# Layer normalisation on one core: the root computed on 128 tokens by 4 and spread by products with scaled identities

## The chip, the core and the metric

The kernel runs on one NeuronCore of a Trainium2 chip. The core has TensorE (PE, matrix products into PSUM; PEld is its weight load), VectorE (DVE), ScalarE (ACT), GpSimd (POOL) and the queue engine SyncE (SP), all working on a shared on-chip memory, SBUF. Time is the device time of one execution in microseconds (us), and the figure compared is the median of several runs.

## The reference

Two transformer blocks are computed for one sequence of 512 tokens with 1024 features. The first block has two layers, and each layer normalises twice, so there are four layer normalisations:

```python
def _layer_norm(x, g, b):
    xf = x.astype(jnp.float32)
    mu = jnp.mean(xf, -1, keepdims=True)
    var = jnp.mean(jnp.square(xf - mu), -1, keepdims=True)
    y = (xf - mu) * lax.rsqrt(var + NORM_EPS)
    return (y * g.astype(jnp.float32) + b.astype(jnp.float32)).astype(x.dtype)
...
    for i in range(DEPTH):
        ...
        x = _layer_norm(DN_ALPHA * x + m, ln1_g[i], ln1_b[i])
        x = _layer_norm(DN_ALPHA * x + _sq_relu_mlp(x, w_up[i], w_down[i]), ln2_g[i], ln2_b[i])
        gate = jax.nn.sigmoid(x @ ple_w_gate[i] + ple_b_gate[i])
        x = x + gate * (p[i] @ ple_w_proj[i])
```

The second block (attention variants, gates, a gated feed-forward part, root-mean-square norms) is not touched.

## The kernel before

Activations are held feature-major: the 128 partitions are features, a row holds the 512 tokens, and 8 such tiles (j = 0 to 7) make the 1024 features. Every large product is split in three: the weight tile and the activation are each written as a rounded high part (WH, XH) and a low part (WL, XL), and high by high, low by high and high by low are summed in a PSUM bank. ACT rounds the weights (L375), DVE subtracts to get the low part (L381, L391), each engine in its own written-out order with semaphores between them.

The four normalisations are called ln1_0, ln2_0, ln1_1 and ln2_1. Their helpers are `ln_pe`, `ln_act`, `ln_pool` and `ln_dve`, one for each engine. Since features lie on partitions, the sums over features come from TensorE: a product with a 128x128 block of ones (ONES) gives the sum for each of the 512 tokens, repeated on all 128 partitions.

- While the residual tiles ACC[:, j] arrive, ACT squares each into X[:, j] (L733) and POOL sums tiles 0 to 6 of both (L787 the values, into SUM1, which the trace calls SM; L791 the squares, into SUM2, which is PT for ln1 and SCR for ln2).
- `ln_pe` makes four f32 products of 512 columns: SUM1 and the last ACC tile into PSUM bank 7 (L697, L699), SUM2 and the last squared tile into bank 6 (L702, L704).
- ACT turns bank 7 into the negative mean (L759, signals `mn`) and squares it (L761). From `mn` on POOL subtracts the mean from tiles 1 to 7, seven operations in a row (L794), and DVE from tile 0 (L798).
- DVE forms the variance for 128x512 elements (L801, L803), ACT takes logarithm and exponential (L763, L765) and a square (L767), DVE makes one Newton step (L806, L808) and leaves the root in bank 6. Then DVE scales the tiles (L814), ACT writes the high part XH with the bias (L775) and DVE the low part XL (L818).
- Meanwhile TensorE runs `proj`, 24 products of 512 columns (four banks, 6 products each, L1231 to L1233) that don't need the normalised tiles. Then comes `lin_pair`: two weight tiles at a time, 48 products (L1294, L1295, L1298), each group as soon as its XH and XL tile are there.

## Time and profile before

| what | value |
|---|---|
| median of 3 runs | 2225.22 us (2224.31 to 2225.51) |
| profiled execution, whole time | 2223.27 us |
| its span from first to last instruction | 2221.4 us |
| TensorE busy | 2173.6 us, 98% of the span |
| VectorE busy | 1237.8 us, 56% |
| ScalarE busy | 896.4 us, 40% |
| GpSimd busy | 220.8 us, 10% |
| mean granted TensorE clock | 1.000 |

Some 1.9 us lie around the span. The shares are averages over a long program; in a normalisation, which takes some ten microseconds, the engines wait for each other in another way than the averages tell.

### The profile page before, as it was taken

Reading aid. Unit: us, or ns where it says so; the run is one execution under the profiler, and the core shown is the slowest. Engines: PE = TensorE matmul, PEld = TensorE weight load, DVE = VectorE, ACT = ScalarE, POOL = GpSimd, SP = SyncE. Lnnn points to the kernel's source line nnn. Section 1 sums busy time; section 2 is a strip of 40 time slices with the busy share of each in tenths; the row PEclk is TensorE's granted clock in tenths of the full one; section 3 lists DMA queues with packets and bytes.
Section 4 is the critical chain, followed back from the end, with each engine's and each line's share of the span. In section 5 each row is a group of like instructions: output and inputs, shape, how many; then the busy total and the mean of one; then the engine's idle time right before and its main releaser. Section 6 shows DMA issues by size and latency. Waiting matters only on the chain.

```text
span 2221.4 us, 27724 instructions
## 1 busy us (share of the span) xinstructions
PE 2173.6 (98%) x10141; PEld 1718.9 (77%) x10141; DVE 1237.8 (56%) x1991; ACT 896.4 (40%) x1498; POOL 220.8 (10%) x145
## 2 busy tenths in 40 slices
PE   8999999999999999999999999999999999999998
PEld 6777788888777777788888777678778787888887
DVE  5676643343474554643344377388489678542554
ACT  4565443233254544433243264432543443321332
POOL 0000400001400001400001320133000231000000
PEclk9999999999999999999999999999999999999999
DMA  6113233333223331333333244123222142333231
GB/s 175 27 46 105 76 94 104 91 98 104 76 77 102 98 96 48 94 95 104 86 98 104 62 135 109 45 86 105 78 61 78 50 121 67 104 104 95 86 104 67
DMA packets 351395, 197.45 MB, mean 89 GB/s; under 512 B 20896, under 2 KB 340141, under 8 KB 351294
## 3 DMA queue, kind: packets, MB, share of 16 engines
q1 hardware_dynamic: 350882, 196.03, 30.9%
q8 instruction: 64, 1.05, 0.2%
q14 instruction: 37, 0.30, 0.0%
q10 hardware_dynamic: 412, 0.07, 0.0%
HBM read 193.93 MB, written 2.14 MB: 88 GB/s over the span
## 4 chain that ended last, share of the span: by engine, by line
PE 85%; DVE 8%; issue 3%; ACT 3%; DMA 0%; POOL 0%; DVEq 0%; SPq 0%; ACTq 0%; POOLq 0%
PE PB L411 20%; PE PB L413 20%; PE PB L412 20%; PE PB L494 3%; PE PB L1407 2%; PE PB L1408 2%; PE PB L1409 2%; PE PB L540 2%; PE PB L513 2%; PE PB L1622 2%; PE PB L1623 2%; PE PB L1624 2%; DVE ATT L2996 1%; DVE WL L381 1%; PE PB L1294 1%
## 5 line engine op out<-in xcount | busy, mean ns | idle before, releaser
L375 ACT ACTIVATE WH<-RAW 128x1024 fp32r<-128x1024 f32 (+3 forms) x355 | 358.3, 1013 | 367.7 <-PE PB L413 273.4
L411 PE MATMUL PB<-XH,WH 128*128 128x512 f32 x1232 | 487.4, 396 | 5.3 <-DVE X L2431 1.3
L413 PE MATMUL PB<-XH,WL 128*128 128x512 f32 x1232 | 480.4, 390 | 0.0
L412 PE MATMUL PB<-XL,WH 128*128 128x512 f32 x1232 | 479.7, 389 | 0.0
L391 DVE TENSOR_TENSOR WL<-RAW,WH 128x1024 fp32r<-128x1024 f32 x172 | 220.7, 1284 | 148.5 <-ACT WH L375 146.6
L411 PEld LDWEIGHTS PB<-XH,WH 128*128 128x128 f32 x1232 | 231.0, 187 | 59.6 <-issue 3.3
L413 PEld LDWEIGHTS PB<-XH,WL 128*128 128x128 f32 x1232 | 230.8, 187 | 49.5
L412 PEld LDWEIGHTS PB<-XL,WH 128*128 128x128 f32 x1232 | 231.1, 188 | 47.1 <-issue 0.7
L381 DVE TENSOR_TENSOR WL<-RAW,WH 128x1024 fp32r<-128x1024 f32 (+2 forms) x163 | 195.6, 1209 | 104.7 <-ACT WH L375 104.0
L413 PE MATMUL PB<-HH,WL 128*128 128x512 f32 x512 | 199.3, 389 | 0.0
L411 PE MATMUL PB<-HH,WH 128*128 128x512 f32 x512 | 199.2, 389 | 0.0
L412 PE MATMUL PB<-HL,WH 128*128 128x512 f32 x512 | 199.2, 389 | 0.0
L2614 DVE TENSOR_SCALAR HR<-PB 128x512 f32<-128x512 f32 x64 | 44.2, 691 | 143.7 <-PE PB L413 143.7
L2038 ACT ACTIVATE HS<-HR 128x512 f32<-128x512 f32 x64 | 40.5, 633 | 190.7 <-DVE HR L2614 190.7
L627 ACT ACTIVATE PT<-PB 128x256 f32<-128x256 f32 (+3 forms) x160 | 65.4, 411 | 120.4 <-PE PB L513 120.4
L411 PEld LDWEIGHTS PB<-HH,WH 128*128 128x128 f32 x512 | 96.1, 188 | 20.0
L413 PEld LDWEIGHTS PB<-HH,WL 128*128 128x128 f32 x512 | 96.1, 188 | 20.0
L412 PEld LDWEIGHTS PB<-HL,WH 128*128 128x128 f32 x512 | 96.1, 188 | 19.9
L787 POOL TENSOR_TENSOR SM<-ACC 128x512 f32<-128x512 f32 x4 | 5.2, 1296 | 1056.6 <-DVE ACC L2600 569.1
L1407 PE MATMUL PB<-XH,WH 128*128 128x512 f32 x256 | 102.9, 402 | 0.4 <-ACT RS L2152 0.4
L1409 PE MATMUL PB<-XH,WL 128*128 128x512 f32 x256 | 99.9, 390 | 0.0
L1408 PE MATMUL PB<-XL,WH 128*128 128x512 f32 x256 | 99.8, 390 | 0.0
(514 smaller groups left out, 3530.2 us busy)
## 6 DMA issues: line engine op xcount, KB each, us to landing
RAW<-in_w_up SPq DMA_DIRECT2D x64, 512.0 KB, 4.0
RAW<-in_w_down SPq DMA_DIRECT2D x64, 512.0 KB, 3.9
RAW<-in_w_ffn_gate_up SPq DMA_DIRECT2D x44, 512.0 KB, 3.8
RAW<-in_w_gate SPq DMA_DIRECT2D x32, 512.0 KB, 4.0
RAW<-in_od_w_in SPq DMA_DIRECT2D x24, 512.0 KB, 6.3
RAW<-in_w_in SPq DMA_DIRECT2D x24, 512.0 KB, 4.1
RAW<-in_w_ffn_down SPq DMA_DIRECT2D x22, 512.0 KB, 3.3
RAW<-in_ple_w_gate SPq DMA_DIRECT2D x16, 512.0 KB, 4.0
```

The costliest lines, as they stand in the source:

```text
L375: act.activation(WH[:, s, 0:nb], RAW[:, s, 0:nb], ACT.Copy).then_inc(hi_done[s], 1)
L381: eng.tensor_tensor(WL[:, s, 0:nb], RAW[:, s, 0:nb], WH[:, s, 0:nb].bitcast(F32), ALU.subtract).then_inc(lo_done[s], 1)
L391: dve.tensor_tensor(WL[:, s], RAW[:, s], WH[:, s].bitcast(F32), ALU.subtract).then_inc(lo_done[s], 1)
L411: pe.matmul(PB[b][0:m, 0:n], WH[:, s, k, 0:m], rh[:, kk, :], start=kk == 0, stop=False)
L412: pe.matmul(PB[b][0:m, 0:n], WH[:, s, k, 0:m], rl[:, kk, :], start=False, stop=False)
L413: x = pe.matmul(PB[b][0:m, 0:n], WL[:, s, k, 0:m], rh[:, kk, :], start=False, stop=kk == last)
L494: xs[e] = pe.matmul(PB[2 + e][:, lo:lo + w], q[:, qb * P:qb * P + P], k[:, ks[0] * P:ks[0] * P + w], start=True, stop=plain)
L513: x = pe.transpose(PB[4 + e][:, c * P:c * P + P], PR[:, e, c * P:c * P + P], ID[:])
L627: done(act.activation(PT[:, e, ks[0]:ks[0] + len(ks), qb * P:qb * P + P], PB[4 + e][:, 0:len(ks) * P].rearrange("p (j q) -> p j q", q=P), ...
L1407: pe.matmul(PB[m % 2][:], WH[:, n % 4, k], XH[:, k], start=k == 0, stop=False)
L1408: pe.matmul(PB[m % 2][:], WH[:, n % 4, k], XL[:, k], start=False, stop=False)
L1409: x = pe.matmul(PB[m % 2][:], WL[:, n % 4, k], XH[:, k], start=False, stop=k == DT - 1)
```

## The change

The variance and the root are computed in another layout: tokens on the 128 partitions, 4 columns (one for each group of 128 tokens). A product whose stationary operand is a 128x128 block of the data and whose moving operand is one column of ones gives the sums for 128 tokens in one PSUM column. Sixteen such products are made for each normalisation (SUM1, SUM2, the last ACC tile, the last squared tile, four blocks each); the two 512-column products of the squares are gone, the two of the mean stay. The chain from variance to root is done on 128x4 elements in STAT. The root then goes back over the features: each of its four columns scales the identity matrix (ID) into a 128x128 block of TMP, two on DVE and two on ACT, and a product of ONES with that block repeats the 128 roots on all partitions. These four products (`ln_spread`) stand in the middle of `proj`, after its first 12 products.

```diff
         def ln_pe(pe, key):
+            sum2, last = SUM2[key[:3]], ACC[:, DT - 1]
+            pe.wait_ge(sem["sum7"], cnt.value("sum7", (key, DT - 2)))
+            for k in range(TT):
+                pe.matmul(PB[6][:, TT + k:TT + k + 1], SUM1[:, k * P:k * P + P], ONES[:, 0:1], start=k == 0, stop=False, skip_group_check=True)
+            pe.wait_ge(sem["sum7q"], cnt.value("sum7q", (key, DT - 2)))
+            for k in range(TT):
+                pe.matmul(PB[6][:, k:k + 1], sum2[:, k * P:k * P + P], ONES[:, 0:1], start=False, stop=False, skip_group_check=True)
             def mean():
-                pe.wait_ge(sem["sum7"], cnt.value("sum7", (key, DT - 2)))
                 pe.matmul(PB[7][:], ONES[:], SUM1, start=True, stop=False)
                 evac_of(pe, M_LN[key] + DT - 1)
-                return pe.matmul(PB[7][:], ONES[:], ACC[:, DT - 1], start=False, stop=True)
+                for k in range(TT):
+                    pe.matmul(PB[6][:, TT + k:TT + k + 1], last[:, k * P:k * P + P], ONES[:, 0:1], start=False, stop=False, skip_group_check=True)
+                return pe.matmul(PB[7][:], ONES[:], last, start=False, stop=True)
             pe_misc(pe, ("mean", key), mean)
-            pe.wait_ge(sem["sum7q"], cnt.value("sum7q", (key, DT - 2)))
-            pe.matmul(PB[6][:], ONES[:], SUM2[key[:3]], start=True, stop=False)
             pe.wait_ge(sem["sqr"], cnt.value("sqr", (key, DT - 1)))
-            done(pe.matmul(PB[6][:], ONES[:], X[:, DT - 1], start=False, stop=True), "varb", key)
+            for k in range(TT):
+                x = pe.matmul(PB[6][:, k:k + 1], X[:, DT - 1, k * P:k * P + P], ONES[:, 0:1], start=False, stop=True, skip_group_check=True)
+            done(x, "varb", key)
+
+        def ln_spread(pe, key):
+            for c, k in enumerate(DIAG_ORDER):
+                wait(pe, "diag_a" if c % 2 else "diag_d", (key, k))
+                x = pe.matmul(PB[6][:, k * P:k * P + P], ONES[:], TMP[:, k * P:k * P + P], start=True, stop=True)
+            done(x, "rootb", key)
...
+        DIAG_ORDER = (0, 2, 1, 3)
+        R0, ROOT = STAT[:, 12:16], STAT[:, 20:24]
         def ln_act(act, key, b, st=None):
...
-            done(act.activation(MEANSQ[key[:3]], MEAN, ACT.Square), "m2", key)
             act.wait_ge(sem["ln_v"], cnt.value("ln_v", key))
-            done(act.activation(RS[:], TMP[:], ACT.Ln), "rs_ln", key)
+            done(act.activation(R0, STAT[:, 8:12], ACT.Ln, bias=EPS5[:]), "rs_ln", key)
...
-            done(act.activation(RS[:], RS[:], ACT.Exp, scale=-0.5), "chain_a", ("rs", key))
-            act.wait_ge(sem["chain_a"], cnt.value("chain_a", ("rs", key)))
-            done(act.activation(PB[7][:], RS[:], ACT.Square), "rs_exp", key)
+            done(act.activation(R0, R0, ACT.Exp, scale=-0.5), "rs_exp", key)
+            act.wait_ge(sem["root"], cnt.value("root", key))
+            for k in DIAG_ORDER[1::2]:
+                done(act.activation(TMP[:, k * P:k * P + P], ID[:], ACT.Copy, scale=ROOT[:, k:k + 1]), "diag_a", (key, k))
...
         def ln_dve(dve, key, g, b):
...
-            done(dve.scalar_tensor_tensor(TMP[:], PB[6][:], 1.0 / D, MEANSQ[key[:3]], ALU.mult, ALU.subtract), "chain_d", ("v", key))
-            done(dve.tensor_scalar(TMP[:], TMP[:], 0.0, 1e-5, ALU.max, ALU.add), "ln_v", key)
+            link(dve.tensor_scalar(q, PB[6][:, TT:2 * TT], -1.0 / D, None, ALU.mult), "m")
+            link(dve.tensor_tensor(q, q, PB[6][:, TT:2 * TT], ALU.mult), "mm")
+            link(dve.tensor_tensor(q, q, PB[6][:, 0:TT], ALU.add), "dv")
+            done(dve.tensor_scalar(v, q, 1.0 / D, 0.0, ALU.mult, ALU.max), "ln_v", key)
             dve.wait_ge(sem["ln_v"], cnt.value("ln_v", key))
+            link(dve.tensor_scalar(v_eps, v, 1e-5, None, ALU.add), "ve")
             dve.wait_ge(sem["rs_exp"], cnt.value("rs_exp", key))
-            done(dve.scalar_tensor_tensor(PB[7][:], PB[7][:], -0.5, TMP[:], ALU.mult, ALU.mult), "chain_d", ("n2", key))
-            done(dve.scalar_tensor_tensor(PB[6][:], PB[7][:], 1.5, RS[:], ALU.add, ALU.mult), "misc_free", ("mean", key))
+            link(dve.tensor_tensor(q, R0, R0, ALU.mult), "n1")
+            link(dve.scalar_tensor_tensor(q, q, -0.5, v_eps, ALU.mult, ALU.mult), "n2")
+            done(dve.scalar_tensor_tensor(ROOT, q, 1.5, R0, ALU.add, ALU.mult), "root", key)
+            dve.wait_ge(sem["root"], cnt.value("root", key))
+            for k in DIAG_ORDER[0::2]:
+                done(dve.tensor_scalar(TMP[:, k * P:k * P + P], ID[:], ROOT[:, k:k + 1], None, ALU.mult), "diag_d", (key, k))
             dve.wait_ge(sem["misc_free"], cnt.value("misc_free", ("mean", key)))
+            dve.wait_ge(sem["rootb"], cnt.value("rootb", key))
...
                 for i in range(4):
+                    if i == 2:
+                        ln_spread(pe, key)
                     for k in range(2):
```

This is what TensorE issues for ln1_0 before, from the end of the layer's output product on; the last row is the first product of `proj`.

```order
L697 MATMUL PB<-SM,ONES 128x512 [waits sum7,misc_free]
L699 MATMUL PB<-ACC,ONES 128x512 [waits evac1]
L702 MATMUL PB<-PT,ONES 128x512 [waits sum7q]
L704 MATMUL PB<-X,ONES 128x512 [waits sqr]
L1231 MATMUL PB<-PTH,WH 128x512 [waits ptev,pt_lo,lo_done0]
```

And this is what it issues in the changed kernel at the same place, and then in the middle of `proj`.

```order
L697 MATMUL PB<-ONES,SM 128x1 [waits sum7]
L700 MATMUL PB<-ONES,PT 128x1 [waits sum7q]
L703 MATMUL PB<-SM,ONES 128x512 [waits misc_free]
L706 MATMUL PB<-ONES,ACC 128x1 [waits evac1]
L707 MATMUL PB<-ACC,ONES 128x512
L711 MATMUL PB<-ONES,X 128x1 [waits sqr]
L1261 MATMUL PB<-PTH,WH 128x512 [waits ptev,pt_lo,lo_done0]
...
L718 MATMUL PB<-TMP,ONES 128x128 [waits diag_d]
L718 MATMUL PB<-TMP,ONES 128x128 [waits diag_a]
```

Each 128x1 row stands for the first of four products. Eight of them, and the wait for the summed squares (`sum7q`), now come ahead of the mean's products, four more between those two. The four spreading products wait for the scaled identities with the second half of `proj` queued behind them.

This is what DVE issues for ln1_0 before, from the mean to the first scaled tiles.

```order
L798 SCALAR_TENSOR_TENSOR ACC<-PB,ACC 128x512 [waits mn]
L801 SCALAR_TENSOR_TENSOR TMP<-PB,PT 128x512 [waits m2,varb]
L803 TENSOR_SCALAR TMP<-TMP 128x512 [waits chain_d]
L806 SCALAR_TENSOR_TENSOR PB<-PB,TMP 128x512 [waits rs_exp,ln_v]
L808 SCALAR_TENSOR_TENSOR PB<-PB,RS 128x512 [waits chain_d]
L814 SCALAR_TENSOR_TENSOR ACC<-ACC,VEC,PB 128x512 [waits misc_free]
```

And this is DVE in the changed kernel.

```order
L815 SCALAR_TENSOR_TENSOR ACC<-PB,ACC 128x512 [waits mn]
L822 TENSOR_SCALAR STAT<-PB 128x4 [waits varb]
L823 TENSOR_TENSOR STAT<-STAT,PB 128x4 [waits chain_d]
L824 TENSOR_TENSOR STAT<-STAT,PB 128x4 [waits chain_d]
L825 TENSOR_SCALAR STAT<-STAT 128x4 [waits chain_d]
L827 TENSOR_SCALAR STAT<-STAT 128x4 [waits ln_v]
L829 TENSOR_TENSOR STAT<-STAT 128x4 [waits rs_exp,chain_d]
L830 SCALAR_TENSOR_TENSOR STAT<-STAT 128x4 [waits chain_d]
L831 SCALAR_TENSOR_TENSOR STAT<-STAT 128x4 [waits chain_d]
L834 TENSOR_SCALAR TMP<-ID,STAT 128x128 [waits root]
L834 TENSOR_SCALAR TMP<-ID,STAT 128x128
L841 SCALAR_TENSOR_TENSOR ACC<-ACC,VEC,PB 128x512 [waits rootb,misc_free]
```

Four wide operations became ten narrow ones. Before, one of the four (L803) has all its operands in SBUF; of the ten, the last seven (L825 to L834) have.

## Rows read from the trace of the kernel before

**Rows 1.** The page: engines' busy time, and the chain that ended last.
```profile
PE 2173.6 (98%) x10141; PEld 1718.9 (77%) x10141; DVE 1237.8 (56%) x1991; ACT 896.4 (40%) x1498; POOL 220.8 (10%) x145
PE 85%; DVE 8%; issue 3%; ACT 3%; DMA 0%; POOL 0%; DVEq 0%; SPq 0%; ACTq 0%; POOLq 0%
```

**Rows 2.** Waits of PE: total us, times, longest.
```profile
PE PB L1294 <- ACT XH L775: 8.0, 7, 1.9
```

**Rows 3.** Timeline of ln2_0: start, length (us), engine, line, tiles, [idle before].
```profile
597.19 1.02 PE L697 MATMUL PB<-SM,ONES 128*128 128x512 f32 x2
...
598.25 1.13 PE L699 MATMUL PB<-ACC,ONES 128*128 128x512 f32 x2
...
599.21 1.02 PE L702 MATMUL PB<-SCR,ONES 128*128 128x512 f32 x2
...
599.41 0.60 ACT L759 ACTIVATE SM<-PB 128x512 f32<-128x512 f32 x1 [0.56 <-PE PB L699]
...
600.04 0.69 DVE L798 SCALAR_TENSOR_TENSOR ACC<-PB,ACC 128x512 f32<-128x512 f32 x1 [1.85 <-ACT SM L759]
600.07 1.02 PE L704 MATMUL PB<-X,ONES 128*128 128x512 f32 x2
...
600.08 8.96 POOL L794 TENSOR_TENSOR ACC<-ACC,SM 128x512 f32<-128x512 f32 x7 [9.17 <-ACT SM L759]
...
606.44 1.41 DVE L814 SCALAR_TENSOR_TENSOR ACC<-ACC,VEC,PB 128x512 f32<-128x512 f32 x2
...
608.05 1.54 DVE L818 SCALAR_TENSOR_TENSOR XL<-ACC,VEC,XH 128x512 fp32r<-128x512 f32 x1 [0.20 <-ACT XH L775]
608.09 0.47 PE L1294 MATMUL PB<-XH,WH 128*128 128x512 f32 x1 [1.51 <-ACT XH L775]
...
619.19 0.84 PE L1298 MATMUL PB<-XL,WH 128*128 128x512 f32 x3
```

**Rows 4.** Timeline of ln1_0, the same columns.
```profile
236.70 1.27 POOL L791 TENSOR_TENSOR PT<-PT,X 128x512 f32<-128x512 f32 x1
...
239.56 8.93 POOL L794 TENSOR_TENSOR ACC<-ACC,SM 128x512 f32<-128x512 f32 x7 [1.59 <-ACT SM L759]
...
247.91 0.47 PE L1294 MATMUL PB<-XH,WH 128*128 128x512 f32 x1 [1.88 <-ACT XH L775]
...
258.60 0.84 PE L1298 MATMUL PB<-XL,WH 128*128 128x512 f32 x3
```

**Rows 5.** Single lines: length min/median/max in ns, first and last start; then POOL's timeline.
```profile
L803 DVE TENSOR_SCALAR TMP<-TMP x4: 1043/1049/1294, 241.3 to 1275.3; 128x512 f32<-128x512 f32 x4
L2845 DVE TENSOR_TENSOR SC<-SC,CHK x3: 294/1264/2385, 1464.2 to 1467.9; 128x128 f32<-128x128 f32 x3
1464.02 3.69 POOL L381 TENSOR_TENSOR WL<-RAW,WH 128x1024 fp32r<-128x1024 f32 x2 [6.35 <-ACT WH L375]
```

**Rows 6.** Timeline of PE where small f32 products follow 512-column ones.
```profile
1716.40 0.39 PE L1408 MATMUL PB<-XL,WH 128*128 128x512 f32 x1
1716.62 0.39 PE L1409 MATMUL PB<-XH,WL 128*128 128x512 f32 x1
1716.85 3.73 PE L1492 MATMUL PB<-XX 128*128 128x128 f32 x32
1720.34 0.48 PE L1407 MATMUL PB<-XH,WH 128*128 128x512 f32 x1
```

**Rows 7.** Timeline of a 128x1 root chain at the program's end.
```profile
2208.05 0.29 ACT L2367 ACTIVATE STAT<-STAT 128x1 f32<-128x1 f32 x1
...
2208.60 0.15 DVE L3182 SCALAR_TENSOR_TENSOR STAT<-STAT 128x1 f32<-128x1 f32 x1
2208.79 0.16 DVE L3184 TENSOR_TENSOR STAT<-STAT 128x1 f32<-128x1 f32 x1
```

**Rows 8.** Clock: last product; window (length, busy, clock, DMA, GB/s); one line's lengths.
```profile
2215.01 0.39 PE L1624 MATMUL PB<-WL,H 128*128 128x512 f32 x1
2220.00:2220.50 0.50, 0.00 (x0) 0.97 0.99 377
L1244 PE MATMUL PB<-ID,XIN x32: 272/421/448, 6.9 to 12.8; 128*128 128x128 f32 x32
```

More of the change, by code:

```diff
@@ L92 @@
  topk hsp hg_x hg_prod hg_read hg_e hg_d hg_o hg_small hx mn m2 varb ln_v x_full sum7q pj pj_free memsum cross xsum
- asum ysum h_up quad mvt yt yo ot_in xt_in z r_tok merge os brf var_out var_in dn dn_free gain_in tok_ss tok_y tok_rt""".split()
+ asum ysum h_up quad mvt yt yo ot_in xt_in z r_tok merge os brf root diag_a diag_d rootb var_out var_in dn dn_free gain_in tok_ss tok_y tok_rt""".split()
 def program(nc, known, t):
@@ L215, in program @@
         SUM2 = {"ln1": PT[:, 0, 0], "ln2": SCR[:, 1]}
-        MEANSQ = {"ln1": PT[:, 0, 1], "ln2": SCR[:, 0]}
         assert max(end_a, end_b, end_c + 4096) <= nc.sbuf_usable_end, (end_a, end_b, end_c, nc.sbuf_usable_end)
@@ L759, in ln_act @@
             done(act.activation(MEAN, PB[7][:], ACT.Copy, scale=-1.0 / D), "mn", key)
-            act.wait_ge(sem["mn"], cnt.value("mn", key))
-            done(act.activation(MEANSQ[key[:3]], MEAN, ACT.Square), "m2", key)
             act.wait_ge(sem["ln_v"], cnt.value("ln_v", key))
-            done(act.activation(RS[:], TMP[:], ACT.Ln), "rs_ln", key)
+            done(act.activation(R0, STAT[:, 8:12], ACT.Ln, bias=EPS5[:]), "rs_ln", key)
             act.wait_ge(sem["rs_ln"], cnt.value("rs_ln", key))
-            done(act.activation(RS[:], RS[:], ACT.Exp, scale=-0.5), "chain_a", ("rs", key))
-            act.wait_ge(sem["chain_a"], cnt.value("chain_a", ("rs", key)))
-            done(act.activation(PB[7][:], RS[:], ACT.Square), "rs_exp", key)
+            done(act.activation(R0, R0, ACT.Exp, scale=-0.5), "rs_exp", key)
+            act.wait_ge(sem["root"], cnt.value("root", key))
+            for k in DIAG_ORDER[1::2]:
+                done(act.activation(TMP[:, k * P:k * P + P], ID[:], ACT.Copy, scale=ROOT[:, k:k + 1]), "diag_a", (key, k))
             if key[:3] == "ln2":
@@ L797, in ln_dve, with link @@
             dve.wait_ge(sem["mn"], cnt.value("mn", key))
-            dve.scalar_tensor_tensor(ACC[:, 0], PB[7][:], -1.0 / D, ACC[:, 0], ALU.mult, ALU.add)
+            done(dve.scalar_tensor_tensor(ACC[:, 0], PB[7][:], -1.0 / D, ACC[:, 0], ALU.mult, ALU.add), "misc_free", ("mean", key))
+            v, q, v_eps = STAT[:, 8:12], STAT[:, 16:20], STAT[:, 24:28]
+            def link(ins, step):
+                done(ins, "chain_d", (step, key))
+                dve.wait_ge(sem["chain_d"], cnt.value("chain_d", (step, key)))
@@ L799, in ln_dve @@
             dve.wait_ge(sem["varb"], cnt.value("varb", key))
-            dve.wait_ge(sem["m2"], cnt.value("m2", key))
-            done(dve.scalar_tensor_tensor(TMP[:], PB[6][:], 1.0 / D, MEANSQ[key[:3]], ALU.mult, ALU.subtract), "chain_d", ("v", key))
-            dve.wait_ge(sem["chain_d"], cnt.value("chain_d", ("v", key)))
-            done(dve.tensor_scalar(TMP[:], TMP[:], 0.0, 1e-5, ALU.max, ALU.add), "ln_v", key)
+            link(dve.tensor_scalar(q, PB[6][:, TT:2 * TT], -1.0 / D, None, ALU.mult), "m")
@@ L807, in ln_dve @@
-            dve.wait_ge(sem["chain_d"], cnt.value("chain_d", ("n2", key)))
-            done(dve.scalar_tensor_tensor(PB[6][:], PB[7][:], 1.5, RS[:], ALU.add, ALU.mult), "misc_free", ("mean", key))
+            link(dve.tensor_tensor(q, R0, R0, ALU.mult), "n1")
+            link(dve.scalar_tensor_tensor(q, q, -0.5, v_eps, ALU.mult, ALU.mult), "n2")
+            done(dve.scalar_tensor_tensor(ROOT, q, 1.5, R0, ALU.add, ALU.mult), "root", key)
+            dve.wait_ge(sem["root"], cnt.value("root", key))
@@ L1218, in proj @@
             def proj(l, o0):
+                key = f"ln{1 if o0 == 0 else 2}_{l}"
                 s, u = st.slot(0)
```

## The prediction

> **What bounds the kernel now.** I read the page first: TensorE is busy for 98% of the span and carries 85% of the last chain [rows 1], so time is won only where TensorE stops, or where it has less to do. Then I read its waits: the largest is that of `lin_pair` for the first normalised tile, 8.0 us in 7 places [rows 2]. So a shorter way from the last residual tile to the first XH tile could win some 1.5 to 1.9 us in each of four normalisations, no more [rows 3, 4]. Then I read the timeline of a normalisation, ln2_0 in full and ln1_0 for what differs. The reader is to see three things there. The four products of the sums take 0.86 us each (L702 to L704). The mean's signal starts POOL on seven subtractions, 8.96 us without a pause, or 1.28 us each; call the start of these P, 600.08 for ln2_0. And `lin_pair` starts at 608.09, P + 8.0 (P + 8.35 in ln1_0). All the root work of DVE lies within POOL's seven operations.
>
> The view that matters most for this change is that of single DVE lines beside POOL [rows 5]. L803 takes 1.05 us, where L798, as wide, takes 0.69. Its start at 241.3 plus 1.05 is 242.35; POOL's second operation ends at 239.56 + 2 x 1.28 = 242.1, and L803 ends 0.25 after it. It has waited for POOL. L818 shows the same: it takes 1.54 us from 608.05, POOL ends at 609.04, and it ends 0.55 later [rows 3]. L2845 shows what happens to several such operations in a row: three of one size (128x128) take 2.385, 1.264 and 0.294 us, beside two POOL operations, the second of which ends at 1467.7. The first of them ends at 1466.6, and so has waited for POOL's first operation. The second ends some 0.15 after 1467.7: POOL's second operation got in between them. Only the third, started at 1467.9 with POOL idle, shows its own length. So two DVE operations that both read SBUF twice don't pass one POOL operation together: the two engines take turns.
>
> The Trainium skill has this as a rule (SBUF — State Buffer, Who interferes with whom): a DVE instruction with two SBUF inputs, or one in a 2-port mode, and a GpSimd instruction lock a shared port pair for their whole length, and the later one blocks fully. The trace agrees, with the 1.264 us of the second L2845 beside 0.294. The Trainium skill (VectorE: DVE Perf Modes, Mode 2×_2P) puts single-source operations in SBUF with an even length among those that lock; no row here shows that for a 4-column one.
>
> **The change, step by step.** The new chain on DVE has seven operations that read and write SBUF only: the variance, its eps, n1, n2, the root, and the two scaled identities. By themselves they are short: links of a chain of one column stand 0.19 us apart [rows 7].
>
> Sums on TensorE: eight loads of f32 weights make a group of four one-column products (two passes each). Thirty-two such passes of 128 columns take 3.49 us, 0.109 each [rows 6], and a pass needs a load of its own whether one column or 128 follow. I take 0.109, so a group costs 0.87 us. Two groups and the products SUM1, then a third group, then the last ACC tile: the mean is later by three groups, 2.6 us. In ln2_0, 0.2 of that is slack, since L699 waited until 598.25 for the last tile where L697 was done at 598.05: 2.4. In ln1_0 the squares' sum, which stood behind the mean, now stands ahead of it, and POOL ends it at 237.97 [rows 4], some 0.3 after the first group: 2.9. So P moves by 2.4 and 2.9.
>
> From P on: DVE takes tile 0 (0.69), then three short operations that read PSUM, so the variance is asked for at P + 1.26, just at POOL's first boundary. Whether it gets in there or at the next, the seven operations meet seven POOL operations: if the first is early, the last goes at the seventh boundary; if not, the last finds POOL done. Seven boundaries of 1.28 are 8.96; with what DVE itself takes in between, the last scaled identity is ready at P + 9.3. ACT's logarithm, exponential and its two identities (0.55 us from L2367 to L3182 [rows 7]) are hidden by these waits. TensorE then makes the last two of the four spreading products: four passes of 0.109, with the signal 0.5, P + 9.8. Then come the 12 products of `proj` that are queued behind them, at 0.227 each [rows 6], 2.7 us: `lin_pair` starts at P + 12.5. The first XH tile is no longer what it waits for: that is 1.65 us after the first L814 [rows 3], and so 1 us before TensorE is through with `proj`.
>
> Sum for ln1_0: 12.5 - 8.35 + 2.9 = 7.05 us later. For ln2_0: 12.5 - 8.0 + 2.4 = 6.9. The third resembles the first without its POOL wait and the fourth the second; I take 6.9 for each. Together 27.8 us. Against it stands the start of `lin_pair`: its 48 products are worth 10.9 us, and they took 11.4 in ln1_0 (247.91 to 258.60 and three products) and 11.8 in ln2_0 (608.09 to 619.19 and three), the stalls behind a late L818. With POOL done and two tiles ahead these go: 2 x (0.45 + 0.85) = 2.6 saved. This leaves 25 us.
>
> The clock: TensorE has nothing from the end of the first half of `proj`, about P + 2.7, until the first scaled identity, at the sixth or seventh boundary, P + 8.0 or P + 9.3. That is 5.3 to 6.6 us. At the program's end the granted clock falls within the window 2220.0 to 2220.5, 5.1 us after the last product [rows 8], from 2.4 to 1.2 GHz. So in some or all of the four the rest of `proj` runs at the lower clock. How slow it is shows at the start, where transposes take 421 ns in the median and 272 at best, until about 12 us, 5 us after the first. Bounds: nothing, or 5 us at half speed, 2.5 us. I take 1.5 for each, 6 together, since the gap is only a little longer than what the end shows. Total 31 us: 2223.27 + 31 = 2254 for the profiled execution, and 2256 for the median, which lies 2 us above it.
>
> **Rivals.**
> *Only two-input operations take turns.* The 4-column variance and eps pass beside POOL; for it speaks that no row shows a narrow single-source operation held. Then five operations wait, the chain ends one boundary earlier, P + 8.0, and the gap on TensorE is 3.9 us, too short for the clock by the row of the end [rows 8]: 25 - 4 x 1.3 = 20, 2245.
>
> *Short operations are not held at all.* For it: L2845 is 128 columns wide, these 4. Against it: its wait is the whole POOL operation, whatever its own length. Then the root is ready by P + 2.6, the identities by P + 3.3, the spreading ends near P + 3.7, and `lin_pair` starts at P + 6.4, 0.8 later than now for ln2_0 with P moved by 2.4. POOL now ends 2.4 us later as well, so one or two more L818 wait for it. About 1 us each: 2229.
>
> *Faster.* If nothing is held, TensorE's work alone decides: 32 loads of a pass x and 0.87 for the spreading come, two products (1.72) and the stall of 1.5 to 1.9 go. The two are even at x = 0.08 us. If a one-column pass costs less than that, the kernel gains; at 0.05 it is 1 us each, 2221. Against it: no f32 load in the trace is so quick behind another, and it needs the rival before it.
>
> *The clock stays low for longer*, into `lin_pair`, or a stall of the same sort comes up elsewhere: above 2266.
>
> **How the numbers follow.** Turns with POOL as forecast 0.66, of which with a clock that never falls (2250) about a third; two-input operations only 0.13; nothing held 0.11; faster 0.04; over 2266 0.06. The forecast's own range is 2248 to 2266. The range reaches down into the second case, 2240, and up to the clock's upper bound, four times 2.5 (2260) with a few us for the mis-sized groups: 2240 to 2265, about 0.8. A measurement of this kernel tells 0.2%, 4.5 us, from no change. The case "nothing held" lies at that border, half in, half out: faster 0.04, same 0.07, slower 0.89.
>
> **What would show it.** In the profile after, POOL's seven subtractions start 2.4 to 2.9 us later in their normalisation than before; beside them the 4-column DVE lines have medians near 1.2 us where their own length is 0.15; the last identity ends 9.3 us after POOL's start; TensorE has a gap of 5 to 7 us in the middle of `proj`, ended by an identity on DVE; `lin_pair` no longer waits for XH; the clock is below 1.0 in windows behind some gaps. The prediction is wrong if the 4-column lines take 0.15 us beside POOL, or if POOL doesn't get in between them.

## The result, and the profile after

The changed kernel takes 2256.35 us (median of 4 executions, 2255.99 to 2257.37) against 2224.89 before (2224.31 to 2225.51), measured side by side: 1.0144 of the time before, with a 95% interval of 1.013 to 1.0159. It is 31.5 us slower. The profiled execution has a span of 2254.6 us, where it was 2221.4.

The page after: busy times, and the clock in 40 slices.

```profile
PE 2197.3 (97%) x10283; PEld 1744.9 (77%) x10285; DVE 1253.1 (56%) x2015; ACT 891.4 (40%) x1498; POOL 219.4 (10%) x145
PEclk9999899999999999999999999999999999999999
```

Its waits of PE. The row of [rows 2] is gone from the list, and this one heads it:

```profile
PE PB L718 <- DVE TMP L834: 16.6, 4, 4.6
```

`lin_pair` no longer waits for its first XH tile; the spreading products wait for the identities that DVE scales, four times, at most 4.6 us. What holds DVE is seen in its single lines (ns, min/median/max; first and last start), in the order of the chain:

```profile
L822 DVE TENSOR_SCALAR STAT<-PB x4: 151/151/163, 244.7 to 1301.6; 128x4 f32<-128x4 f32 x4
L825 DVE TENSOR_SCALAR STAT<-STAT x4: 190/190/1123, 245.2 to 1302.2; 128x4 f32<-128x4 f32 x4
L827 DVE TENSOR_SCALAR STAT<-STAT x4: 1199/1217/1217, 246.4 to 1302.4; 128x4 f32<-128x4 f32 x4
L829 DVE TENSOR_TENSOR STAT<-STAT x4: 1182/1182/1200, 247.6 to 1303.7; 128x4 f32<-128x4 f32 x4
L831 DVE SCALAR_TENSOR_TENSOR STAT<-STAT x4: 1183/1186/1186, 250.1 to 1306.1; 128x4 f32<-128x4 f32 x4
L834 DVE TENSOR_SCALAR TMP<-ID,STAT x8: 273/1250/1308, 251.3 to 1308.5; 128x128 f32<-128x128 f32 x8
```

L822 and L827 do the same kind of work on the same 128x4 elements. The one reads PSUM and takes 0.15 us; the other reads and writes SBUF and takes 1.22. The timeline of ln2_0 after, to be laid beside [rows 3], shows why:

```profile
606.80 0.95 PE L697 MATMUL PB<-ONES,SM 128*128 128x1 f32 x8
607.61 1.03 PE L700 MATMUL PB<-ONES,SCR 128*128 128x1 f32 x8
...
612.07 8.65 POOL L811 TENSOR_TENSOR ACC<-ACC,SM 128x512 f32<-128x512 f32 x7 [11.54 <-ACT SM L777]
...
613.20 0.19 DVE L825 TENSOR_SCALAR STAT<-STAT 128x4 f32<-128x4 f32 x1
613.43 1.22 DVE L827 TENSOR_SCALAR STAT<-STAT 128x4 f32<-128x4 f32 x1
...
614.61 0.39 PE L1263 MATMUL PB<-PTH,WL 128*128 128x512 f32 x1
614.68 1.18 DVE L829 TENSOR_TENSOR STAT<-STAT 128x4 f32<-128x4 f32 x1
...
617.11 1.19 DVE L831 SCALAR_TENSOR_TENSOR STAT<-STAT 128x4 f32<-128x4 f32 x1
618.33 2.47 DVE L834 TENSOR_SCALAR TMP<-ID,STAT 128x128 f32<-128x128 f32 x2
...
619.63 2.44 PE L718 MATMUL PB<-TMP,ONES 128*128 128x128 f32 x8 [4.64 <-DVE TMP L834]
...
621.73 0.77 PE L1261 MATMUL PB<-PTH,WH 128*128 128x512 f32 x1
```

POOL's seven operations take 8.65 us, 1.236 each, so its second ends at 614.54 and its third at 615.78. L827 ends at 614.65 and L829 at 615.86: each narrow operation ends 0.1 us behind one of POOL's. The second identity ends at 620.80, behind the seventh (620.72). TensorE ran out of products at 615.00 and waits until 619.63.

The clock in that stage, and in ln1_0 (windows: length, then busy time of PE, PEld, DVE, ACT, POOL, then granted clock, DMA share and GB/s):

```profile
616.00:618.00 2.00, 0.00 (x0) 0.00 (x0) 1.97 (x2) 0.00 (x0) 2.00 (x2) 1.00 0.00 0
618.00:619.00 1.00, 0.00 (x0) 0.00 (x0) 0.96 (x2) 0.67 (x2) 1.00 (x2) 0.84 0.00 0
622.00:624.00 2.00, 2.00 (x6) 1.53 (x5) 1.60 (x3) 1.02 (x2) 0.00 (x0) 0.50 0.00 0
626.00:628.00 2.00, 2.00 (x11) 1.61 (x10) 2.00 (x4) 0.84 (x2) 0.00 (x0) 1.00 0.00 0
...
238.00:240.00 2.00, 2.00 (x13) 1.52 (x13) 0.00 (x0) 0.00 (x0) 0.00 (x0) 0.95 0.00 0
240.00:242.00 2.00, 2.00 (x7) 1.55 (x8) 0.00 (x0) 0.00 (x0) 0.00 (x0) 0.50 0.00 0
```

In ln2_0 the clock falls to half (1.2 GHz) inside the gap, after 618, and `proj` runs at it until 625.5, which is almost all of its rest. In ln1_0 it falls at another place as well: at 239.8, while TensorE is shown busy with the one-column products. The prediction has nothing of that.

The four normalisations hold the whole loss. From the first product of the sums to the end of `lin_pair` (its last product counted with the 0.227 us at which products follow each other) they took 22.4, 22.7, 22.75 and 22.65 us (90.5 together) and now take 32.3, 30.4, 30.6 and 30.6 (123.9): 33.5 us more by the unrounded times, where the span grew by 33.2. These sums of four stages are used below for each kernel.

### The profile page after: what moved, and what is told of

The parts are those of the page before. It is cut to its first block, busy times and chain, and to the rows that moved or that the text cites. A ratio compares the mean times of both kernels' runs of the same rounds, so it can differ in the third digit from the quotient of the medians.

```text
span 2254.6 us, 28030 instructions
## 1 busy us (share of the span) xinstructions
PE 2197.3 (97%) x10283; PEld 1744.9 (77%) x10285; DVE 1253.1 (56%) x2015; ACT 891.4 (40%) x1498; POOL 219.4 (10%) x145
## 4 chain that ended last, share of the span: by engine, by line
PE 86%; DVE 8%; issue 3%; ACT 2%; DMA 0%; POOL 0%; DVEq 0%; SPq 0%; ACTq 0%; POOLq 0%
PE PB L410 20%; PE PB L412 20%; PE PB L411 20%; PE PB L493 2%; PE PB L1437 2%; PE PB L1438 2%; PE PB L1439 2%; PE PB L539 2%; PE PB L512 2%; PE PB L1654 2%; PE PB L1653 2%; PE PB L1652 2%; PE PB L1324 1%; PE PB L1325 1%; PE PB L1328 1%
```

## The experiments

### The turns with POOL

**POOL starts later (e1_pool_waits).** One line of the changed kernel: POOL's subtractions wait for the last identity of DVE instead of the mean.

```diff
         def ln_pool(pool, key, b):
...
-            pool.wait_ge(sem["mn"], cnt.value("mn", key))
+            pool.wait_ge(sem["diag_d"], cnt.value("diag_d", (key, 1)))
```

> The changed kernel with one edit: POOL starts its seven subtractions only when DVE has written both scaled identities. Every DVE operation is the same. Turn-taking theory: the 4-column lines L825 to L831 take 0.15 to 0.19 us each (1.18 to 1.22 before this edit), the identities 0.27, and the gap in the middle of proj shrinks from about 5 us to 1.3 or less, so the clock stays at 1.0 there. POOL and DVE's L845 now take turns later, 1 to 3 us for each normalisation. Time 2226 to 2240, middle 2233. Rival, the narrow chain is slow by itself (ten linked operations and two hops to ACT): the lines keep about 1.2 us or the gap stays over 4 us, and the time stays above 2250.

Measured: 2237.31 us (2234.48 to 2238.55), 1.0059 [1.0043, 1.0074] of the time before; four stages 99.9 us. Two of its lines:

```profile
L829 DVE TENSOR_TENSOR STAT<-STAT x4: 162/164/165, 246.2 to 1287.4; 128x4 f32<-128x4 f32 x4
L845 DVE SCALAR_TENSOR_TENSOR XL<-ACC,VEC,XH x32: 737/1118/1673, 251.9 to 1302.6; 128x512 fp32r<-128x512 f32 x32
```

With POOL idle the same instruction takes 0.164 us, not 1.182. So the length that it had was POOL's. In ln2_0 the pause in the middle of `proj` is gone, and the stage takes 24.3 us instead of 30.4; some 2 of these 6 are the clock, which no longer falls behind a gap there (e3 below). The kernel gets 19 us back. In ln1_0 the clock still falls in the sums, at 241.3. Part of the price is moved: POOL's work now lies beside L845, whose median goes from 0.74 to 1.12.

**Half as wide on POOL (e8_pool_halves).** The same subtractions as 14 operations of 256 columns.

```diff
-                done(pool.tensor_tensor(ACC[:, j], ACC[:, j], MEAN, ALU.add), "cen", (key, j))
+                pool.tensor_tensor(ACC[:, j, 0:256], ACC[:, j, 0:256], MEAN[:, 0:256], ALU.add)
+                done(pool.tensor_tensor(ACC[:, j, 256:512], ACC[:, j, 256:512], MEAN[:, 256:512], ALU.add), "cen", (key, j))
```

> The changed kernel with POOL's seven subtractions cut into fourteen of 256 columns. Nothing on DVE, ACT or TensorE is edited. Turn-taking theory: a turn costs one POOL operation, so the narrow DVE lines fall from 1.18 to about 0.6 us, the chain from POOL's start to the second identity from 8.7 to about 4.7 us, the gap in proj closes but for 1.5 us and the clock stays up behind it. L845 then meets POOL's second half. About 5.5 us less in each normalisation, 2234 (2230 to 2240). Rival, a narrow operation waits for POOL's whole queue or for a fixed time: the lines keep 1.2 us and the time stays at 2255 to 2258.

Measured: 2239.71 us (2239.29 to 2241.15), 1.0072 [1.0055, 1.0088]; four stages 105.0 us. The chain's lines, one number further on, and POOL's:

```profile
L830 DVE TENSOR_TENSOR STAT<-STAT x4: 647/659/659, 247.1 to 1290.1; 128x4 f32<-128x4 f32 x4
L831 DVE SCALAR_TENSOR_TENSOR STAT<-STAT x4: 646/646/656, 247.8 to 1290.8; 128x4 f32<-128x4 f32 x4
L811 POOL TENSOR_TENSOR ACC<-ACC,SM x28: 712/734/1237, 244.3 to 1296.2; 128x256 f32<-128x256 f32 x28
```

The DVE instructions are unchanged, and go from 1.18 to 0.65 us with POOL's. A wait for POOL's whole instruction explains both; a fixed cost of a narrow operation explains neither. The second identity ends 5.6 us after POOL's start in ln2_0, where it was 8.7. The clock still falls in ln1_0's sums and, in ln1_1, at 929.5, behind a gap of 2.1 us.

**The chain through PSUM (e2_psum_chain).** POOL starts as in the change. Each DVE operation has at most one operand in SBUF; the square of R0 and all four identities are ACT's.

```diff
-            link(dve.tensor_tensor(q, q, PB[6][:, 0:TT], ALU.add), "dv")
-            done(dve.tensor_scalar(v, q, 1.0 / D, 0.0, ALU.mult, ALU.max), "ln_v", key)
+            link(dve.tensor_tensor(qp, q, PB[6][:, 0:TT], ALU.add), "dv")
+            done(dve.tensor_scalar(v, qp, 1.0 / D, 0.0, ALU.mult, ALU.max), "ln_v", key)
...
-            link(dve.tensor_scalar(v_eps, v, 1e-5, None, ALU.add), "ve")
+            link(dve.tensor_scalar(v_eps, qp, 1.0 / D, 1e-5, ALU.mult, ALU.add), "ve")
...
-            link(dve.tensor_tensor(q, R0, R0, ALU.mult), "n1")
-            link(dve.scalar_tensor_tensor(q, q, -0.5, v_eps, ALU.mult, ALU.mult), "n2")
-            done(dve.scalar_tensor_tensor(ROOT, q, 1.5, R0, ALU.add, ALU.mult), "root", key)
+            link(dve.scalar_tensor_tensor(qp, PB[6][:, 8:12], -0.5, v_eps, ALU.mult, ALU.mult), "n2")
+            done(dve.scalar_tensor_tensor(ROOT, qp, 1.5, R0, ALU.add, ALU.mult), "root", key)
...
```

> The changed kernel with the chain's operands placed so that no DVE operation between the mean and the root reads SBUF twice or goes from SBUF to SBUF (two of its small arrays lie in PSUM, ACT squares the root's first estimate), and with all four scaled identities on ACT. POOL starts at the mean as in the changed kernel. Turn-taking theory: the narrow lines take about 0.15 to 0.2 us beside POOL, the four identities 0.35 each on ACT, the gap in proj is 1 to 2 us, the clock stays up there; L845 still waits for POOL at first, as in the kernel before. Per normalisation some 2 us more than before the change, 2233 (2229 to 2238). Rival, narrow operations are held by POOL wherever their operands lie: lines near 1.2 us, over 2248.

Measured: 2233.78 us (2232.25 to 2235.44), 1.0042 [1.0026, 1.0057]; four stages 99.6 us, three of them 23.9; in ln1_0 the clock fell in the sums, at 239.8.

```profile
L830 DVE TENSOR_SCALAR STAT<-PB x4: 161/161/161, 245.3 to 1284.7; 128x4 f32<-128x4 f32 x4
L832 DVE SCALAR_TENSOR_TENSOR PB<-PB,STAT x4: 170/170/171, 246.2 to 1285.6; 128x4 f32<-128x4 f32 x4
L814 POOL TENSOR_TENSOR ACC<-ACC,SM x28: 1270/1288/1743, 243.7 to 1290.9; 128x512 f32<-128x512 f32 x28
```

Beside POOL operations of 1.29 us the chain now runs at its own length. The single operands tell the two rules apart: L827 of the changed kernel has one operand, in SBUF, and waits; L830 here has one, in PSUM, and doesn't. The Trainium skill (SBUF — State Buffer, Who interferes with whom) says that a DVE instruction with at most one SBUF input, outside the 2-port modes, doesn't contend with GpSimd. The trace agrees, with 0.16 to 0.17 us.

**Two identities back on DVE (e6_psum_dve_ids).** e2, with the two even blocks scaled by DVE again, from ID in SBUF into TMP in SBUF.

```diff
...
-            for k in DIAG_ORDER:
+            for k in DIAG_ORDER[1::2]:
...
+            for k in DIAG_ORDER[0::2]:
+                done(dve.tensor_scalar(TMP[:, k * P:k * P + P], ID[:], ROOT[:, k:k + 1], None, ALU.mult), "diag_d", (key, k))
```

> As the kernel with the chain's operands in PSUM, but two of the four identities are made by DVE again, from SBUF to SBUF. Turn-taking theory: these two, and only these, take turns with POOL, 1.2 us each where they take 0.28 alone; the spreading ends 1 to 1.5 us later than there, and L845 meets less of POOL afterwards: some 1 us more per normalisation, 2237 (2235 to 2241). Rival, ACT's four identities in a row were the slow part: the same time as there or less, 2231 to 2234.

Measured: 2239.64 us (2237.26 to 2239.94), 1.0066 [1.0049, 1.0083]; four stages 104.8 us.

```profile
L836 DVE TENSOR_SCALAR TMP<-ID,STAT x8: 962/1284/1322, 250.4 to 1292.8; 128x128 f32<-128x128 f32 x8
```

Two turns are back, 1.28 us for work of 0.28, and the stages are 5.2 us longer than in e2. In ln2_0 `lin_pair` starts 8.4 us after POOL instead of 7.0, and is itself 0.6 shorter: 0.85 in all, and as much in ln1_1. That is the price of the two turns. In ln1_0 and ln2_1 the difference is 1.6 and 1.9, and there the clock has a part: it was low in ln1_0 from 239.5 to 253.1, where in e2 it was back at 250.1, and in ln2_1 it fell in the sums, as it didn't in e2.

**The mean's products first (e4_mean_first).** The changed kernel with the groups on SUM1 and SUM2 moved behind the products of the mean. This takes back more than half of the delay of POOL's start and leaves the turns.

```diff
...
             pe_misc(pe, ("mean", key), mean)
+            for k in range(TT):
+                pe.matmul(PB[6][:, TT + k:TT + k + 1], SUM1[:, k * P:k * P + P], ONES[:, 0:1], start=False, stop=False, skip_group_check=True)
+            pe.wait_ge(sem["sum7q"], cnt.value("sum7q", (key, DT - 2)))
+            for k in range(TT):
+                pe.matmul(PB[6][:, k:k + 1], sum2[:, k * P:k * P + P], ONES[:, 0:1], start=False, stop=False, skip_group_check=True)
...
```

> The changed kernel with the one-column groups of SUM1 and SUM2 moved behind the mean's two products (the group of the last tile stays ahead of the second). The products are the same. The mean, and with it POOL's start, comes 1.6 us earlier, the variance at the same time as in the changed kernel. Turn-taking theory: two of POOL's seven operations are over before the first DVE operation that needs SBUF twice, so the last identity escapes a turn, the chain ends about 1.2 us earlier than in the changed kernel: 2251 (2247 to 2253). Rival, the order of the groups is what the path pays for in full, 1.6 us each: 2249.5; if POOL's start sets nothing: 2256.

Measured: 2246.03 us (2243.84 to 2248.7), 1.0102 [1.0085, 1.0119], below the expected range; four stages 111.1 us. POOL starts 3.8 us after the first product in ln2_0 instead of 5.3. The chain starts later against POOL, so five of its operations wait for a turn where six did, and the identities find POOL done:

```profile
L834 DVE TENSOR_SCALAR TMP<-ID,STAT x8: 281/284/288, 249.1 to 1299.0; 128x128 f32<-128x128 f32 x8
```

The last identity ends 13.0 us after the stage's first product, where it was 14.0: an earlier POOL by 1.5 us is worth 1.0. But the stage is 3.0 us shorter (27.45 for 30.4), and `lin_pair` starts 12.8 us after POOL, where it was 14.3. The other 2 us are the clock's. In all four stages it fell in the sums or right behind them, and in ln2_0 it was up again when the rest of `proj` ran, which in the change runs at half clock:

```profile
610.00:614.00 4.00, 4.00 (x11) 3.03 (x11) 3.83 (x6) 0.50 (x2) 4.00 (x4) 0.50 0.00 0
616.00:618.00 2.00, 1.57 (x11) 1.49 (x12) 0.83 (x4) 1.90 (x3) 0.03 (x1) 1.00 0.00 0
```

The slow part then lies in the first half of `proj`, and even so TensorE is through with that half 1.4 us before the first identity comes.

### The clock

**Work in the gap (e3_fill).** The changed kernel with five 512-column products, whose result is not used, ahead of the spreading products.

```diff
                     if i == 2:
+                        wait(pe, "misc_free", ("mean", key))
+                        for c in range(5):
+                            pe.matmul(PB[7][:], ONES[:], X[:, c], start=True, stop=True)
                         ln_spread(pe, key)
```

> The changed kernel with five f32 products of 512 columns put into PSUM bank 7, which nobody reads, ahead of the spreading products, 4.3 us of work in TensorE's gap of 4.6 us. Nothing waits for them. If the low clock after the gap is a part of the loss, the granted clock stays 1.0 behind the gaps of ln2_0, ln1_1 and ln2_1, the second half of proj takes 0.227 us a product and the time falls by 2 to 3 us in each of the three, to 2248 (2246 to 2251); ln1_0, where the clock falls ahead of the gap, may keep its loss. Rival, the clock costs nothing because the next phase waits for XL anyway: 2255 to 2257.

Measured: 2253.23 us (2252.22 to 2254.37), 1.0128 [1.0113, 1.0144]; four stages 119.0 us. The median is above the expected 2246 to 2251, and only one of the three stages did what was expected. In ln2_0 the clock stays up, and the stage takes 28.25 us instead of 30.43: the clock's price behind the gap is 2.2 us. But ln1_1 and ln2_1 gain only 0.5 each, since there the clock now falls ahead of the gap. Windows of ln2_0, ln1_1 and ln2_1:

```profile
612.00:616.00 4.00, 4.00 (x14) 2.30 (x13) 3.87 (x4) 0.50 (x2) 4.00 (x4) 1.00 0.00 0
620.00:624.00 4.00, 4.00 (x20) 3.31 (x19) 3.50 (x6) 2.03 (x3) 0.00 (x0) 1.00 0.01 2
926.00:930.00 4.00, 4.00 (x16) 2.73 (x15) 0.89 (x1) 0.45 (x1) 0.00 (x0) 0.61 0.68 195
1298.00:1302.00 4.00, 4.00 (x12) 3.23 (x12) 3.65 (x7) 0.50 (x2) 4.00 (x4) 0.50 0.61 185
```

In 926:930 TensorE is at the products of the sums, busy all 4 us, and the clock is at 0.61; in ln2_1 it fell in the sums too, and 1298:1302 shows it still low. In neither does TensorE pause for more than 0.2 us in the 8 us before the fall, so a gap can't be the reason there.

**Everything put right but the width (e7_psum_order).** e2's chain and identities, e4's order, and the spreading after 18 products of `proj` in place of 12. No turn is left, and TensorE pauses for 0.4 us at most.

```diff
...
-                    if i == 2:
+                    if i == 3:
                         ln_spread(pe, key)
```

> A version of the changed kernel with what the first runs pointed to: chain operands in PSUM, all identities on ACT, the mean's products ahead of two of the one-column groups, and the spreading after 18 products of proj where it stood after 12. POOL starts 1.6 us earlier, no gap is left in proj, L845 waits for POOL less. Per normalisation 22.9 us from the first sum to the end of lin_pair, where the kernel before takes 22.7 and the version with PSUM operands alone 23.9: 2226 (2223 to 2229). It would not beat the kernel before, since the sixteen one-column products and the four spreading ones cost TensorE 4.1 us and only 1.7 of products and 1.7 of waiting are saved.

Measured: 2236.39 us (2236.3 to 2236.58), 1.0055 [1.0038, 1.0071]; a miss by 10 us. ln1_0 took 23.4 us, ln2_0 26.8, ln1_1 26.7, ln2_1 25.2: with TensorE busy throughout, the clock fell in the last three. Hence the next kernel.

**64 columns of ones (e9_psum_order_64).** e7, with the moving operand of the one-column products 64 columns wide. The number of loads and products is the same; DVE reads one column in 64.

```diff
-                pe.matmul(PB[6][:, k:k + 1], sum2[:, k * P:k * P + P], ONES[:, 0:1], start=False, stop=False, skip_group_check=True)
+                pe.matmul(PB[6][:, k * 64:(k + 1) * 64], sum2[:, k * P:k * P + P], ONES[:, 0:64], start=False, stop=False, skip_group_check=True)
...
-            link(dve.tensor_scalar(q, PB[6][:, TT:2 * TT], -1.0 / D, None, ALU.mult), "m")
+            link(dve.tensor_scalar(q, PB[6][:, 256:512:64], -1.0 / D, None, ALU.mult), "m")
...
```

> e7_psum_order with the same loads and the same number of products, but each of the last block's sums and of the means and squares goes against 64 columns of ones instead of one (vector operations read one column in 64). My theory, formed after e7: a stretch of one-column products lets the clock fall, although TensorE is shown busy; with 64 columns it stays at 1.00, each of the four stages takes the 23.4 us that ln1_0 took in e7 at clock 1.00 (plus at most 0.3 for wider products), 4 x 23.6 = 94.4 against 90.5 before, 2227 to 2230. Rival: the clock falls whatever the width, from the loads or from what follows; then the three stages keep 25.2 to 26.8 us and it is 2235 to 2238, as e7.

Measured: 2227.48 us (2227.12 to 2231.25, 10 executions), 1.0018 [1.0009, 1.0028]; the stages take 23.4, 23.6, 23.5 and 23.6 us. The same window of ln2_0, first in e7:

```profile
602.00:606.00 4.00, 4.00 (x20) 3.90 (x20) 1.22 (x5) 0.03 (x1) 3.90 (x4) 0.54 0.00 0
```

and then in e9:

```profile
602.00:606.00 4.00, 4.00 (x30) 3.74 (x30) 1.50 (x6) 1.12 (x4) 3.38 (x3) 1.00 0.00 0
```

In both TensorE is busy for the 4 us, and gets through 20 products in the one and 30 in the other. Products 64 times as wide cost next to nothing (8 passes take 0.8 to 0.9 us either way), and the kernel is 8.9 us faster. 8.0 of these lie in the four stages; about one more lies in the second block, where the clock of e7's profiled execution was low from 1745.8 to 1749.2, behind a gap of 2.3 us, and that of e9 wasn't.

**One column and 64, in the kernel before (e10_before_16, e11_before_16x64).** To have the width alone, without any of the change: the kernel before, with 16 products more between those of the mean and those of the squares, whose result is not used. The diff of e10; in e11 the moving operand is `ONES[:, 0:64]` and the result 64 columns wide.

```diff
             pe_misc(pe, ("mean", key), mean)
             pe.wait_ge(sem["sum7q"], cnt.value("sum7q", (key, DT - 2)))
+            for c in range(16):
+                pe.matmul(PB[6][:, c:c + 1], SUM1[:, c % 4 * P:c % 4 * P + P], ONES[:, 0:1], start=c == 0, stop=c == 15, skip_group_check=True)
```

> The kernel before (sum and mean products as they were) with 16 more one-column products per normalisation, whose result is not used, between the products of the mean and those of the squares. At the measured pitch of 0.2 us for the load and product of a pair (0.203 with loads) they add 16 x 0.203 = 3.25 us, 13 in all: 2238 if the clock holds. If a stretch of one-column products lets the clock fall: 1 to 3 us more in each, 2241 to 2249, and the clock row shows the fall inside or right behind the stretch.

> As e10_before_16, but the 16 added products have 64 columns of ones each. Both theories: about the same work, 13 us (2238 to 2239) while the clock is 1.00. If one-column products are what lets it fall, this one holds the clock and is 3 to 10 us faster than e10_before_16; if the clock doesn't mind the width, both are the same.

Measured: 2240.7 us (2238.99 to 2241.28), 1.007 [1.0053, 1.0087], with one column; 2237.17 (2235.35 to 2237.25), 1.0054 [1.0037, 1.007], with 64. In ln1_0 both stages take 25.7 us. In the other three e10 takes 26.8 to 27.0 and e11 25.6 to 25.7: 3.6 us in all, and the medians differ by 3.5. In ln2_0 the 16 products stand at 602.8 to 606.4; the windows of e10:

```profile
603.00:605.00 2.00, 2.00 (x21) 2.00 (x20) 0.69 (x1) 1.23 (x2) 1.29 (x2) 1.00 0.00 0
605.00:607.00 2.00, 2.00 (x15) 1.84 (x15) 0.00 (x0) 0.00 (x0) 2.00 (x2) 0.82 0.00 0
607.00:609.00 2.00, 2.00 (x3) 0.67 (x2) 0.00 (x0) 0.00 (x0) 2.00 (x3) 0.50 0.00 0
```

and those of e11, where they start 0.3 us earlier:

```profile
605.00:607.00 2.00, 2.00 (x15) 1.52 (x14) 0.00 (x0) 0.00 (x0) 2.00 (x2) 1.00 0.00 0
607.00:609.00 2.00, 2.00 (x9) 1.31 (x7) 0.92 (x2) 0.00 (x0) 2.00 (x3) 1.00 0.00 0
```

The clock falls at the end of a stretch of one-column products (606.3), with no gap and none of the change there; with 64 columns it doesn't.

**64 columns in the changed kernel (e12_after_64).** The same replacement in the changed kernel and nothing else.

> The changed kernel itself, with 64 columns of ones in place of one in the four groups of products. It parts the two ways in which the clock falls. My theory: the turns with POOL leave the gap of 4.6 us as it is, so the clock still falls in the gap at all four places and the first part of the rest of proj runs at half speed; only what the one-column products cost goes: in ln1_0, where the clock fell inside them, the time from the first sum product to POOL's start is 5.3 instead of 7.3 us, in the three others the stage stays at 30.4 to 30.7. All in all 2 us less: 2254 to 2255. Rival: the one-column products also bring the fall in the gap forward or keep the clock low behind it; then each of the four is 1 to 2 us shorter, 2248 to 2252, and the clock falls later than 3.7 us after the last product.

Measured: 2257.37 us (2253.11 to 2259.48, 4 executions), 1.015 [1.0133, 1.0167], outside what either theory expected. By the median this shows nothing; the executions lie 6 us apart. The profiled one (span 2251.3) is the fastest of the four, and two others had a lower mean clock (0.991 against 0.994); these were not profiled. It bears out the first theory: ln1_0 took 29.75 us instead of 32.3, its clock being 1.00 through the sums (5.7 us to POOL's start instead of 7.3), and the others 29.9, 30.4 and 30.5 instead of 30.4, 30.6 and 30.6. The clock falls in the gap as before, in ln2_0 at 615.3, 2.7 us after the last product:

```profile
240.00:242.00 2.00, 2.00 (x15) 1.52 (x14) 0.00 (x0) 0.25 (x1) 0.00 (x0) 1.00 0.00 0
...
616.00:618.00 2.00, 0.76 (x3) 0.76 (x4) 2.00 (x2) 1.91 (x3) 2.00 (x2) 0.50 0.00 0
```

### A version that beats both

**The logarithm past the waiting operation (e5_wide_early_log).** The kernel before, wide as it was. The trace of before shows L803 waiting for POOL (1.05 us, [rows 5]) with ACT's logarithm behind it. Here the logarithm reads L801's result with eps as its bias, and L803 runs beside it into another tile. The logarithm's argument is no longer clamped at zero first; the kernel leaves out nothing else.

```diff
...
-            done(act.activation(RS[:], TMP[:], ACT.Ln), "rs_ln", key)
+            done(act.activation(RS[:], TMP[:], ACT.Ln, bias=EPS5[:]), "rs_ln", key)
...
-            done(dve.scalar_tensor_tensor(TMP[:], PB[6][:], 1.0 / D, MEANSQ[key[:3]], ALU.mult, ALU.subtract), "chain_d", ("v", key))
+            done(dve.scalar_tensor_tensor(TMP[:], PB[6][:], 1.0 / D, MEANSQ[key[:3]], ALU.mult, ALU.subtract), "ln_v", key)
+            dve.wait_ge(sem["ln_v"], cnt.value("ln_v", key))
+            done(dve.tensor_scalar(VT[:], TMP[:], 0.0, 1e-5, ALU.max, ALU.add), "chain_d", ("v", key))
             dve.wait_ge(sem["chain_d"], cnt.value("chain_d", ("v", key)))
-            done(dve.tensor_scalar(TMP[:], TMP[:], 0.0, 1e-5, ALU.max, ALU.add), "ln_v", key)
-            dve.wait_ge(sem["ln_v"], cnt.value("ln_v", key))
             dve.wait_ge(sem["rs_exp"], cnt.value("rs_exp", key))
-            done(dve.scalar_tensor_tensor(PB[7][:], PB[7][:], -0.5, TMP[:], ALU.mult, ALU.mult), "chain_d", ("n2", key))
+            done(dve.scalar_tensor_tensor(PB[7][:], PB[7][:], -0.5, VT[:], ALU.mult, ALU.mult), "chain_d", ("n2", key))
...
```

> The kernel before, wide chain, with one edit: ACT takes the logarithm straight from L801's result with 1e-5 as its bias (as the changed kernel does), and L803, which waits 0.8 us for POOL, runs beside ACT's work and no longer ahead of it. The root is 1.05 us earlier in each normalisation, of which TensorE's wait for the first XH tile (1.5 to 1.9 us) gives back about 1: 2221 (2219 to 2223). Rival: L818 then meets POOL one operation earlier and waits longer, and the lin_pair phase gives it all back: 2224 to 2226. The output uses no lower clamp of the variance inside the logarithm.

Measured: 2222.03 us (2219.82 to 2222.75, 11 executions) against 2224.92 (15), 0.9987 [0.9978, 0.9996]; the stages take 21.5, 21.75, 21.9 and 21.75 us, 3.6 less in all. The gain is 0.13%, and the interval ends just short of no gain; the stages, one profiled execution of each kernel, say the same. In ln2_0:

```profile
600.49 0.69 DVE L801 SCALAR_TENSOR_TENSOR TMP<-PB,SCR 128x512 f32<-128x512 f32 x1 [0.40 <-PE PB L704]
601.21 1.05 DVE L803 TENSOR_SCALAR VT<-TMP 128x512 f32<-128x512 f32 x1
601.21 0.73 ACT L763 ACTIVATE RS<-TMP,EPS 128x512 f32<-128x512 f32 x1 [1.18 <-DVE TMP L801]
```

L803 waits for POOL as long as ever, and nobody waits for L803. `lin_pair` starts at 606.46, 7.0 us after POOL instead of 8.0.

## Why the prediction was right

The forecast was 2256.0, the median is 2256.35. That is closer than its steps deserve: they were off in opposite directions.

*POOL starts later by 2.4 and 2.9.* Right where the clock was up: the first product to POOL's start went from 2.89 to 5.27 in ln2_0. A pass with one column took 0.101 to 0.111 us (0.81 for the eight of L697, 0.89 for those of L700) for the forecast's 0.109. In ln1_0 it went from 2.67 to 7.27. In e12, with the clock up there, it is 5.7, so 3.0 of the 4.6 are the products and the wait for the squares' sum, as forecast, and 1.6 the clock.

*Seven operations meet seven operations of POOL.* Shown, and by e1, e8 and e2 from three sides. The first got in at POOL's first boundary (L825, 0.19 us in three of the four), and the last, the second identity, ended at P + 8.73. The forecast had P + 9.3, with POOL's operation at 1.28 us for a measured 1.236 and some 0.3 us of DVE's own.

*The rest of `proj` is queued behind, `lin_pair` at P + 12.5.* Its form was right. From P + 8.73 the last spreading products would end near P + 9.2 at the full clock and `lin_pair` start at P + 12.0, an estimate from passes of 0.109 us and products of 0.227 (in ln2_0 of e3, with the clock up, it was P + 12.1); in ln1_0, where the second identity ended at P + 8.92, at P + 12.2. It started at P + 14.13 to P + 14.47, and what lies between is the clock's.

*`lin_pair` saves 2.6.* It saved 3.05 (10.9 us in all four for 11.4 to 11.8).

*The clock, 1.5 in each.* The mis-sized term. Against P + 12.2 and P + 12.0 the four pay 1.9, 2.3, 2.4 and 2.5 us behind the gap, and ln1_0 another 1.6 in its sums: 10.7 us instead of 6. e3 measured the part behind the gap of ln2_0 by itself: 2.2. The forecast took the end of the program, 5.1 us without a product, for what the clock needs to fall, and so thought a gap of 5.3 to 6.6 only just long enough. The gap itself was shorter than that, 4.6 us in three stages and 2.7 in ln1_0, since the first identity came at the sixth boundary and its product started at P + 7.56; and the clock fell all the same, in ln2_0 at 618.7, 3.7 us after the last product. The upper bound that it named, 2.5 us, was nearly the truth. Without the clock the sum is 33.5 - 10.7 = 22.8, where the forecast had 25; so 2.2 too much for the rest and 4.7 too little for the clock made 31 for a measured 33.5. What brought the median so close was the last step, the 2 us added between the profiled execution and the median: there was no such distance after (2256.44 against 2256.35).

*The rivals.* That only two-input operations take turns fell with L827, which has one operand and took 1.22 us. Its sum also took a gap of 3.9 us for too short for the clock; the clock fell 3.7 us after the last product here and 2.7 in ln2_0 of e12. That short operations are not held fell with the same rows. "Faster" needed a pass of under 0.08 us and got 0.101 at best; and e9, with no turn, no gap and the clock at 1.00 in the four stages, is still 3.5 us slower than the kernel before. So the change would not have paid even without what went wrong: it gives TensorE, which bounds the kernel, more to do. The stalls of `lin_pair` that it removes are worth less.

## What to carry to other kernels

A narrow DVE operation from SBUF to SBUF costs its own 0.16 us only while POOL is idle; in a chain beside POOL each link costs a whole POOL instruction (1.2 us here), so count links, not elements. Put the chain's operands in PSUM, or give the links to ACT, or let the next engine read past the link that waits (e5). Before moving the last link of a chain onto TensorE, see what is queued behind it there, and count the clock twice: for the gap, and for a stretch of very narrow products.
